# Latent projections of layer 1 placed between the expert slots of layer 0's two context tiles

## The reference

```
for l in range(2):
    need_ctx = l < 1
    sh1, sc1, g1, sh2, sc2, g2 = modulation(c)          # and csh1 ... cg2 for context
    ux, uc = x * (1 + sc1) + sh1, ctx * (1 + csc1) + csh1
    px, pc = ux @ w_in[l], uc @ w_in[l]                 # columns: qk, v, o, gates, nq, nk, nv
    yx, yc = mixer(px, pc)                              # conv on qk, mLSTM heads, window attention
    x = LN(ALPHA * x + g1 * (yx @ w_out))               # context the same if need_ctx
    x = LN(ALPHA * x + g2 * peer(x * (1 + sc2) + sh2))  # context the same if need_ctx
return x
peer(u): for each token and each of 8 heads: two score rows of 128 keys, top 16 of each,
    top 16 of their 256 sums, softmax; y += gate * gelu(u . up[e]) * down[e]
```

## Time and profile before

| | us |
|---|---|
| median of 3 runs | 4351.84 |
| lowest and highest run | 4351.81, 4360.9 |
| span of the profiled execution | 4349.6 |
| last expert slot of layer 0 done, first job of layer 1's projections (PE L718) | 2577.5 |
| last `head_scores` of layer 1's projection stage done | 2818.4 |
| PE, DVE, ACT, POOL busy | 3807.1, 2820.5, 1699.8, 1935.9 |

### The profile page before, as it was taken

The page is one execution under the profiler, slowest core; times in us unless marked ns, Lnnn a source line. Parts: engine busy times, 40 slices in busy tenths (PEclk is TensorE's granted clock), DMA queues, the critical chain, the costliest instruction groups (busy, mean ns, idle before and its releaser), DMA issues. The chain is left out here.

```text
span 4349.6 us, 45764 instructions
## 1 busy us (share of the span) xinstructions
PE 3807.1 (88%) x11520; PEld 1731.8 (40%) x11520; DVE 2820.5 (65%) x6967; ACT 1699.8 (39%) x4746; POOL 1935.9 (45%) x1425
## 2 busy tenths in 40 slices
PE   7999899888888888888888889989988888888887
PEld 3445554433333333333333335465443333333332
DVE  3105867777777777777777643176776776777775
ACT  2012514444444444444444432143544444444443
POOL 1110115556556556556556530011555655655555
PEclk9999999999999999999999999989999999999999
DMA  7641249999999999999999981225999999999998
GB/s 286 218 143 51 110 168 418 421 421 421 421 415 416 419 417 412 420 413 419 414 413 420 414 314 44 63 81 199 380 421 422 421 419 421 414 415 417 411 422 334
DMA packets 243627, 1486.54 MB, mean 342 GB/s; under 512 B 24960, under 2 KB 49792, under 8 KB 72688
## 3 DMA queue, kind: packets, MB, share of 16 engines
q0 software_dynamic: 191232, 1385.58, 77.5%
q1 hardware_dynamic: 52208, 98.79, 6.6%
HBM read 1477.87 MB, written 2.21 MB: 340 GB/s over the span
## 5 line engine op out<-in xcount | busy, mean ns | idle before, releaser
L934 PE MATMUL psum<-arena 128*128 128x512 f32 x5120 | 2503.9, 618 | 450.9 <-ACT arena L1195 426.4
L1308 POOL DMA_INDIRECT arena<-in_updown,arena x1280 | 1846.0, 1442 | 1584.6 <-PE psum L934 1062.5
L1744 DVE CUSTOM_DVE_ANT_0 arena<-arena 128x1024 bf16<-128x1024 f32 x1276 | 1567.0, 1228 | 877.3 <-DMA arena<-in_updown,arena 773.1
L934 PEld LDWEIGHTS psum<-arena 128*128 128x128 f32 x5120 | 892.0, 191 | 1790.6 <-ACT arena L1195 1076.5
L1201 ACT ACTIVATE arena<-arena 128x1 f32<-128x1 f32 x1280 | 259.4, 203 | 1660.8 <-DVE arena L1744 1657.0
L1195 ACT ACTIVATE arena<-CN,arena 128x128 f32<-128x128 f32 x1280 | 513.9, 402 | 45.7
L1191 ACT ACTIVATE arena<-arena 128x1 f32<-128x1 f32 x1280 | 376.7, 294 | 73.9 <-ACT arena L1201 5.4
L898 PE MATMUL psum<-arena 128*128 128x256 f32 (+1 forms) x1280 | 362.7, 379 | 3.0 <-ACT arena L1166 1.6
L898 PEld LDWEIGHTS psum<-arena 128*128 128x128 f32 x1280 | 242.4, 190 | 257.2 <-issue 251.4
L1301 POOL TENSOR_TENSOR arena<-arena 128x256 f32<-128x256 f32 x64 | 50.1, 814 | 516.4 <-DMA arena<-in_bias 516.4
L740 PE MATMUL psum<-arena 128*128 128x512 f32 (+1 forms) x672 | 237.6, 510 | 4.4 <-DMA arena<-in_w_in 2.4
(11 more groups left out here) (196 smaller groups left out, 2578.2 us busy)
## 6 DMA issues: line engine op xcount, KB each, us to landing
arena<-in_ada_w POOLq DMA_DIRECT2D x40, 1024.0 KB, 5.4
arena<-in_updown,arena POOLq DMA_INDIRECT x1280
arena<-in_wq SPq DMA_DIRECT2D x16, 1024.0 KB, 18.4
arena<-in_w_in SPq DMA_DIRECT2D x6, 2048.0 KB, 9.7
arena<-in_w_in SPq DMA_DIRECT2D x24, 512.0 KB, 4.4
arena<-in_ada_w SPq DMA_DIRECT2D x4, 2048.0 KB, 14.4
arena<-in_bias SPq DMA_DIRECT2D x16, 512.0 KB, 3.6
arena<-in_w_out SPq DMA_DIRECT2D x2, 4096.0 KB, 13.0
```

Of the source, the lines that this page charges most:

```text
L934: mm = e.matmul(ps[ACCUMULATORS[t % 2][hf]][:], diag[:, k % DIAGS, :], ring[k % RING][:, D + hf * 512:D + (hf + 1) * 512], start=first, st ...
L1308: e.indirect_dma_start(ring[k % RING], None, updown, bass.IndirectOffsetOnAxis(ap=idx16[:, k:k + 1], axis=0)).then_inc(sem(f"rows{k % RING ...
L1744: e.tensor_tensor_reduce(prod[:, k % 2, :], ring[k % RING][:, 0:D], u, 1.0, 0.0, ALU.mult, ALU.add, dots[:, k:k + 1]).then_inc(sem("expert ...
```

## The change

Five sections of 512 columns of `w_in[1]` (NQ, NK, V, O and ML, that is attention queries and keys, mLSTM values and output gates, and the conv input) are multiplied with the latent tokens during the expert slots of layer 0's tiles 4 and 5. Each section is eight slices of one 128-row block (256 KB, rows of 2048 bytes, `wslice`, four buffers), and each slice is four pieces, one for each of four banks (2 to 5), of one 512-column matmul. `ahead_plan` puts one piece ahead of `weigh` in each slot from tile 4, unit 4, slot 2 on, leaves out three of 16 slots (k = 3, 8, 13) and two slots after each section. That places 146 of the 160 pieces in 190 slots; the other 14 run after the last slot (`ahead_late`). ACT copies the four banks of a closed section out one slot after another (`keep_piece`). The sixth latent projection (B) stays.

So that banks and SBUF are free, all 16 heads' key scores of tiles 4 and 5 are made earlier (`SCORE_PLAN`, from tile 3, unit 5 to tile 4, unit 3, in banks 2 and 3) and are copied by ACT to SBUF (`keep_score`), where `route` reads them; tile 5's `u` is modulated in unit 0 of tile 4 and turned at its slot 14. The eight latent turns of X stand in tile 4, unit 3, slots 8 to 15 (`turn_x`, `keep_x`). Tiles 4 and 5 and the last units of tile 3 are written out in place of loops. The `wq_ahead`, `turn_ahead` and `keep_ahead` code goes. In layer 1 the first T job waits for all 20 copied banks; the convolution inputs of all four chunks lie in `raw4`, so that `conv(0)` and `conv(1)` start at the first G job, `gates` stands at job M 2, and `conv(2)`, `conv(3)` at job X; ACT applies the sigmoid to the copied gates `sigo` after the V jobs.

```diff
+    if l:
+        jobs += [("T", k, "c", "va"[k % 2]) for k in range(KD)]
+        for g in range(2):
+            jobs += [("G", g, "x", "a"), ("G", g, "c", "a")]
+        jobs += [("M", 2, "c", "a"), ("M", 3, "c", "a"), ("R", 0, "x", "v"), ("R", 1, "x", "v"), ("K", 0, "c", "a"), ("K", 1, "c", "a"),
+                 ("X", 0, "x", "v"), ("K", 2, "c", "a"), ("R", 2, "x", "v"), ("K", 3, "c", "a"), ("R", 3, "x", "v")]
+        jobs += [("V", t, "c", "va"[t % 2]) for t in range(NCT)]
...
+SCORE_PLAN = {(CTX_AT - 1, 5): ((0,), 5, 13), (CTX_AT - 1, 6): ((1, 2), 0, 16), (CTX_AT - 1, 7): ((3, 4), 0, 16),
+              (CTX_AT, 0): ((5, 6, 7), 0, 14), (CTX_AT, 1): ((8, 9, 10), 2, 16), (CTX_AT, 2): ((11, 12, 13), 0, 16),
+              (CTX_AT, 3): ((14, 15), 0, 8)}
+SCORE_SLOTS = 5
+LAST_TURN_AT = 14
+TURN_X = (CTX_AT, 3, 8)
+FIRST_AHEAD = (CTX_AT, 4, 2)
+AHEAD_SKIP = (3, 8, 13)
+SECTION_GAP = 2
...
+def ahead_plan():
+    at, late, kept = {}, [], {}
+    free = [n for n in range(slot_number(*FIRST_AHEAD), NT * PH * TOPK) if n % TOPK not in AHEAD_SKIP]
+    for x in range(len(SECTIONS)):
+        for y in range(KD * PIECES):
+            if free:
+                at[free.pop(0)] = (x, y // PIECES, y % PIECES)
+                end = max(at)
+            else:
+                late.append((x, y // PIECES, y % PIECES))
+        if x < len(SECTIONS) - 1:
+            for a in range(PIECES):
+                kept[end + 1 + a] = (x, a)
+            free = free[SECTION_GAP:]
+    return at, late, kept
...
-                    for c in range(4):
-                        done = next(k for k in range(TOPK) if wq_at + (c + 1) * KD * P <= wo_at + (k + 1) * 2 * D)
-                        e.wait_ge(sem("experts.slot_done"), NT * PH * TOPK - RING + MIX_SLOTS + done + 1)
-                        e.dma_start(wq_ahead[:, c], wv[:, :, COL_NQ + c * P:COL_NQ + (c + 1) * P]).then_inc(sem(f"wq_ahead_loaded{c}"), 16)
+                    e.wait_ge(sem("experts.key_mm"), NT * PH)
+                    for j in range(len(SECTIONS) * KD):
+                        if j >= SLICES:
+                            e.wait_ge(sem("ahead.slice_mm"), j - SLICES + 1)
+                        col = SECTIONS[j // KD]
+                        e.dma_start(wslice[:, j % SLICES], wv[:, j % KD, col:col + 512]).then_inc(sem(f"ahead.slice_loaded{j % SLICES}"), 16)
...
+                    if l and n == 0:
+                        e.wait_ge(sem("ahead.kept"), PIECES * len(SECTIONS))
+                        e.wait_ge(sem("experts.tile_done"), NT)
...
+                def ahead_score(n, k):
+                    if k == 0:
+                        if n == 0:
+                            e.wait_ge(sem("experts.route_read"), CTX_AT * PH + 1)
+                        if n >= 2:
+                            e.wait_ge(sem("ahead.score_kept"), n - 1)
+                        if n == PH:
+                            e.wait_ge(sem("experts.uT_ready"), CTX_AT + 2)
+                    key_score(n % PH, ps[2 + n % 2], k)
+                def turn_x(k):
+                    if k == 0:
+                        e.wait_ge(sem("experts.tile_done"), CTX_AT)
+                    if k >= 2:
+                        e.wait_ge(sem("ahead.u_kept"), k - 1)
+                    for a in range(NT - NCT):
+                        mm = e.transpose(ps[4 + k % 2][:, a * P:(a + 1) * P], X[:, NCT + a, k * P:(k + 1) * P], ident)
+                    mm.then_inc(sem("ahead.turned"), 1)
+                def section_mm(x, k, a):
+                    j = x * KD + k
+                    if a == 0:
+                        e.wait_ge(sem(f"ahead.slice_loaded{j % SLICES}"), 16 * (j // SLICES + 1))
+                    if x == 0 and k == 0:
+                        if a < 2:
+                            e.wait_ge(sem("ahead.score_kept"), 2 * PH - 1 + a)
+                        else:
+                            e.wait_ge(sem("ahead.u_kept"), KD - 3 + a)
+                    if x == 0 and a == 0:
+                        e.wait_ge(sem("ahead.u_kept"), k + 1)
+                    if x >= 1 and k == 0:
+                        e.wait_ge(sem("ahead.kept"), PIECES * (x - 1) + a + 1)
+                    bank, w = ps[2 + a][:], wslice[:, j % SLICES, :]
+                    if SECTIONS[x] in (COL_V, COL_O):
+                        mm = e.matmul(bank, uTx[:, k, a * P:(a + 1) * P], w, start=(k == 0), stop=(k == KD - 1), skip_group_check=True)
+                    else:
+                        mm = e.matmul(bank, w[:, a * P:(a + 1) * P], uTx[:, k, :], start=(k == 0), stop=(k == KD - 1), skip_group_check=True)
+                    if a == PIECES - 1:
+                        mm.then_inc(sem("ahead.slice_mm"), 1)
+                def ahead_unit(t, h):
+                    un = t * PH + h
+                    for k in range(TOPK):
+                        if (t, h, k) == (CTX_AT, 0, LAST_TURN_AT):
+                            turn_u(CTX_AT + 1)
+                        for n, kk in scores_in_slot(t, h, k):
+                            ahead_score(n, kk)
+                        if (t, h) == TURN_X[0:2] and 0 <= k - TURN_X[2] < KD:
+                            turn_x(k - TURN_X[2])
+                        if slot_number(t, h, k) in ahead_at:
+                            section_mm(*ahead_at[slot_number(t, h, k)])
+                        weigh(t, un * TOPK, k, h == 0 and k == 0, h == PH - 1 and k == TOPK - 1)
...
+                if q_ctx:
+                    for x, k, a in ahead_late:
+                        section_mm(x, k, a)
...
+                    if l and kind == "M" and i == 3:
+                        silu(0)
+                        silu(1)
+                        gates_exp()
+                    if l and kind == "K" and i == 1:
+                        silu(2)
+                    if l and kind == "K" and i == 2:
+                        silu(3)
+                    if l and kind == "V" and i == NCT - 1:
+                        e.wait_ge(sem("ahead.kept"), PIECES * len(SECTIONS))
+                        for t in range(NCT, NT):
+                            e.activation(sigo[:, t, :], sigo[:, t, :], ACT.Sigmoid)
...
+                def keep_score(n):
+                    e.wait_ge(sem("experts.key_mm"), CTX_AT * PH + n + 1)
+                    if SCORE_SLOTS <= n < PH:
+                        e.wait_ge(sem("experts.route_read"), CTX_AT * PH + n - SCORE_SLOTS + 2)
+                    e.activation(kept_score(n), ps[2 + n % 2][:, 0:2 * NKEY].rearrange("p (f n) -> p f n", f=2), ACT.Copy).then_inc(sem("ahead.score_kept"), 1)
...
+                def keep_x(k):
+                    e.wait_ge(sem("ahead.turned"), k + 1)
+                    e.activation(uTx[:, k, :], ps[4 + k % 2][:], ACT.Identity, scale=mod_scalar(l + 1, SC1, k, 1),
+                                 bias=mod_scalar(l + 1, SH1, k, 1)).then_inc(sem("ahead.u_kept"), 1)
+                def keep_piece(x, a):
+                    e.wait_ge(sem("ahead.slice_mm"), KD * (x + 1))
+                    bank = ps[2 + a][:]
+                    if SECTIONS[x] == COL_NQ:
+                        ins = e.activation(nq_grid(l + 1, a), bank.rearrange("p (r b c) -> p r b c", r=ROWS, b=NBAND), ACT.Copy, scale=DH ** -0.5)
+                    elif SECTIONS[x] == COL_NK:
+                        ins = e.activation(nk[:, a, CTX:T], bank, ACT.Copy)
+                    elif SECTIONS[x] == COL_V:
+                        e.wait_ge(sem("experts.route_read"), (CTX_AT + 1) * PH + VML_SCORES + 1)
+                        ins = e.activation(vml[:, NCT + a, :, 0:DV], bank.rearrange("p (h d) -> p h d", h=MLH), ACT.Copy)
+                    elif SECTIONS[x] == COL_O:
+                        ins = e.activation(sigo[:, NCT + a, :], bank, ACT.Copy)
+                    else:
+                        ins = e.activation(raw4[:, a, 262:262 + SEQ], bank, ACT.Copy)
+                    ins.then_inc(sem("ahead.kept"), 1)
...
+                    if not more and q_ctx:
+                        e.wait_ge(sem("experts.slot_done"), NT * PH * TOPK)
+                        for a in range(PIECES):
+                            keep_piece(len(SECTIONS) - 1, a)
...
+                    else:
+                        if kind == "G" and i == 0 and part == "x":
+                            conv(0)
+                            conv(1)
+                        if kind == "M" and i == 2:
+                            gates()
+                        if kind == "X":
+                            conv(2)
+                            conv(3)
...
+                        if q_ctx and isinstance(un, int) and un >= CTX_AT * PH:
+                            e.wait_ge(sem("ahead.score_kept"), un - CTX_AT * PH + 1)
+                            e.sem_inc(sem("experts.dve_token"), 1)
+                            S = [kept_score(un - CTX_AT * PH)[:, hf] for hf in range(2)]
```

364 lines of the change are left out of this document (215 added, 149 removed).

## The result

| | before | after |
|---|---|---|
| median of 4 runs, us | 4353.85 | 4275.43 |
| lowest and highest, us | 4351.81, 4360.9 | 4273.43, 4283.28 |
| span of the profiled execution, us | 4349.6 | 4270.8 |

The ratio is 0.9816, with a 95% interval of 0.9804 to 0.9827. The forecast was 4267, in a range of 4244 to 4300: the gain of the medians is 78.4 us, where 85 were forecast (the median of before rose by 2 us with a fourth run).

The account below looks back on a forecast made before the run. Gathers were taken to bound the expert stage and PE the projection stage. 4349.6 - 114.5 (projection stage) + 29.2 (slices) = 4264.3 us of span; 2.2 us to the median gave 4267 us, range 4244 to 4300.

Parts of the forecast that it names:

- The bound of the slots: Layer 0's expert slots: gathers set the pace at 2.52 us a slot, about 2.67 with slices; PE has room.
- The price of the slices: Expert slots from tile 4: 39 weight slices at 0.75 us each add 29.2 us.
- the fuller PE: Expert slots: PE's added work counts nothing in the sum, 0 to 4 us in the range.
- The projection stage: Layer 1, last expert slot to last head scores: 240.8 us falls to 126.3, giving back 114.5 us.
- T at +14.5: Layer 1's projections: first T job starts 14.5 us after the last slot, once late pieces' banks are copied.
- X at +46.4: Layer 1's projections: X can start 46.4 us after the last slot, set by the gates' chain; PE waits 5 us.
- B at +74.5: Layer 1's projections: V ends 74.5 us after the last slot; B and head scores then take 48.8 us.
- the 3 us for slow stretches: Layer 1's projections: allowance of 3 us for PE at a lower clock after waits, raising +123.3 to +126.3.
- PE at the pace of the slots: Rival for the expert slots: PE needs 44.9 us a unit against 42.8 of DMA; 25 us more, 4292; chance 0.10.
- Slices dearer than their bytes: Rival for the expert slots: gathers stall 2.2 us for each slice, 57 us more, 4324; chance 0.05.
- Pieces that lengthen their slot: Rival for the expert slots: each piece adds 0.86 us to its slot, 126 us for 146, total 4363; chance 0.05.
- slices would fill time of the gathers not bound by bytes: Rival for the expert slots: slices use gather time not byte-bound, or projection waits are shorter; 15 us less, 4252; chance 0.10.

Follow-up runs that it names:

- half pieces: Changed kernel with only 256 of the 512 result columns of each piece computed; 3686.0 us from the first gather, against 3686.4.
- thin slices: Changed kernel with only 32 of 512 columns of slices 4 to 39 loaded, all matmuls kept; 3668.1 us from the first gather, against 3686.4.
- double slices: Changed kernel with each slice loaded twice into the same buffer, one load after the other; 3713.8 us from the first gather, against 3686.4.
- double pieces: Changed kernel with each piece's matmul done twice into the same bank; 3773.4 us from the first gather, against 3686.4.

## Why the prediction was right

**The bound of the slots was right.** Gathers bound by bytes, and PE with room for a piece: half pieces left the spacing at 2.66 us and thin slices took it to 2.54. The spacing forecast was 2.67.

**The price of the slices was right, a little dear**: 29.2 us forecast, +30.1 measured from the first gather to the end of the last slot. Taken apart, 35 slices cost 24.9 us (0.71 each), four more some 3, and the remaining 2.4 are within the 0 to 4 us that I had given to the fuller PE in the range and not in the sum. So the agreement within 0.9 us is partly luck: the slices alone came to 24 to 28 us, by the 0.62 us of a second load or the 0.71. What was paid was bytes: these prices for 256 KB are 423 and 369 GB/s. My 0.75 came from 350 GB/s in a window of the kernel before (2593 to 2598.5 us) that also holds the start of a load, the first microsecond of which shows 30 to 268 GB/s; in full flow such rows ran at 386 GB/s beside G in the changed kernel, which would be 0.68 us.

The Trainium skill (DMA: Bandwidth & Descriptors, Measured (HBM→SBUF, 128 partitions, SWDGE, issued from GpSimd)) has 341 GB/s for 1 MB and 138 GB/s for 64 KB, from which 0.77 to 1.90 us for a slice was the estimate in the prediction. Its dear end, 76 us for 40 slices, did not come: beside a queue that kept the engines busy all the time, the slots took 30 us longer.

**The projection stage was right**: 126 us forecast, 127.9 measured, against 240.8. Step by step: T at +14.5 forecast and +14.4 measured; X at +46.4 and +51.0; B at +74.5 (without the 3 us for slow stretches) and +79.3; B's stretch 48.8 and 48.7. The difference arises in G, where I took 5.95 us from the kernel before and 11.9 were needed. ACT's logarithm of the gates and their second exponential after the change:

```profile
2645.63 0.84 ACT L1261 ACTIVATE arena<-arena 8x768 f32<-8x768 f32 x1
...
2661.96 0.84 ACT L1209 ACTIVATE arena<-arena 8x768 f32<-8x768 f32 x1
```

From G's start to the logarithm's end it was 17.2 us (2629.27 to 2646.47) where I had 12.7, and from there to the exponential's end 16.3 us, as forecast. Of the 5.95 us more in G, 3.28 are the pause, 1.65 the lower clock of its second half and 1.0 a longer wait behind it. The pause stands nowhere in my sum. PE waited 3.28 us ahead of X, not 5, because G's excess delayed it more than the chain, and 0.44 us ahead of R 2, not 3, because K 2's slow rows filled that wait. The 3 us that I had added for the lower clock covered most of the excess in G, so the total was nearer than its parts, by luck.

**What missed.** The gain was 78.8 us of span in place of 85.3. Of the 6.5 us, 4.4 lie ahead of the first gather, where the kernels are the same and executions differ by up to 12 us; this isn't a step of the sum but its frame: I compared one execution's span with the runs' medians and gave that frame no uncertainty. The other 2 us are the slots' 0.9 and the stage's 1.6, less 0.3 behind it. The gain of the medians isn't firm to this either: it was 78.4 us in the first series and 84.0 in the last one (4359.93 and 4275.89).

**The rivals.** PE at the pace of the slots is refuted by the half pieces; the double pieces show where it would begin. Slices dearer than their bytes are refuted by the double slices. Pieces that lengthen their slot did not appear. The double ones do so, as a full PE and not as a blocked one: the last slot ends 105 us later than before, 0.72 us for each of 146, their late pieces take 12 us more, and with that the gain is gone (3773.4 us from the first gather against 3769.6 of before). That slices would fill time of the gathers not bound by bytes was not seen either: the rate in the slots stayed at 414 GB/s, and no slice came out cheaper than its bytes at 421 GB/s (0.62 us).

## What to carry to other kernels

Where one stage is bound by transfers and the next by matmuls, matmuls moved into the first cost little but the bytes that they bring, as long as the engine's sum per period stays below the transfers' period (here 2.38 us against 2.66, with a ring of eight buffers between them); compute both sums from start-to-start distances of back-to-back instructions, not from their printed durations. What is saved in the second stage is less than the work taken out, since what it covered (here the gates' chain over DVE and ACT) comes to light; look there for independent jobs to put in. And compare single profiles between two points that hold what changed, and leave out the parts that vary by themselves: here up to 12 us ahead of the first gather and 5 us behind the last head scores.

## What the runs showed of the hardware

- A queue of 2048-byte rows beside a saturated queue of 8192-byte rows cost 0.62 to 0.71 us for each 256 KB, and the total rate stayed at 413 to 414 GB/s with each slice loaded once or twice.
- PE stood 3.28 us with nothing to wait for that the profile shows, while 4 MB of loads were under way at 386 GB/s; with those loads held back the same place took 0.99 us. Over the twelve profiles of changed kernels it was 3.2 to 3.8 us with the loads and 0 to 1.7 without. The next 128 rows took 4.48 us at a granted clock of 0.60 and 0.65, instead of 2.83 at 1.00.
- After 9.27 us without work PE ran 16 transposes at a granted clock of 0.50, the level of 1.2 GHz, in 3.68 us. After 2.22 us without work they stood at 1.00 and took 1.97 in one kernel, and at 0.54 and took 3.51 in another.
- The same program ahead of the first gather took 580.0 to 592.3 us over thirteen executions, with a mean granted clock of 0.97 to 0.95.
